# Attention of 24 score maps in one order of steps: scores a step earlier, one bias ahead of a division, even exponentials first

## Time and profile before

| | |
|---|---|
| runs of the kernel | 2519.49, 2513.41, 2519.65 us (median 2519.49) |
| profiled execution | 2518.29 us, its span 2516.5 us |
| granted clock of PE, mean | 0.999 |
| PE busy | 99% of the span |
| DVE, ACT, GpSimd busy | 61%, 54%, 10% |
| attention of layer 0 / layer 1 of block 2 | starts near 1562.7 / 2164.8 us of the span |

### The profile page before, as it was taken

How to read it: one execution, slowest core, us unless ns; L and a number is a source line. 1 busy time by engine, 2 the same in 40 slices (tenths; PEclk the granted TensorE clock), 3 DMA queues, 4 the chain that set the end, 5 groups by cost and what they waited for, 6 DMA issues and landing times.

```text
span 2516.5 us, 47973 instructions
## 1 busy us (share of the span) xinstructions
PE 2479.6 (99%) x19246; PEld 2312.7 (92%) x19246; DVE 1531.5 (61%) x2036; ACT 1346.9 (54%) x2077; POOL 255.5 (10%) x164
## 2 busy tenths in 40 slices
PE   9999999999999999999999999999999999999998
PEld 8989998999999999899989989799989988888997
DVE  5658756565565774656656556566555655567654
ACT  5447555544544664655555445665445445565543
POOL 0200220000000002100100001460000000354000
PEclk9999999999999999999999999999999999999999
DMA  6655414465655552348656555345555655434654
GB/s 235 207 186 172 136 67 160 143 197 195 198 198 193 168 166 70 126 142 228 205 178 202 194 177 161 110 145 187 188 189 186 195 193 168 135 111 167 201 188 139
DMA packets 118382, 428.10 MB, mean 170 GB/s; under 512 B 13164, under 2 KB 14956, under 8 KB 117804
## 3 DMA queue, kind: packets, MB, share of 16 engines
q1 hardware_dynamic: 117696, 424.82, 51.8%
q10 hardware_dynamic: 492, 0.46, 0.1%
HBM read 423.79 MB, written 1.44 MB: 169 GB/s over the span
## 4 chain that ended last, share of the span: by engine, by line
PE 92%; DVE 4%; ACT 2%; issue 1%; DMA 0%; ACTq 0%; SPq 0%; DVEq 0%; POOLq 0%
PE bank L483 41%; PE bank L694 39%; PE bank L503 2%; PE bank L1004 2%; PE bank L1708 1%; PE bank L1104 1%; DVE lo_slots L471 1%; PE bank L633 1%; PE bank L1725 1%; PE bank L1751 1%; PE bank L1895 1%; PE bank L1871 1%; DVE rope_mem L2108 1%; ACT hi_slots L457 0%; ACT probs L1790 0%
## 5 line engine op out<-in xcount | busy, mean ns | idle before, releaser
L471 DVE TENSOR_TENSOR lo_slots<-raw,hi_slots 128x1024 fp32r<-128x1024 f32 x732 | 901.1, 1237 | 696.3 <-ACT hi_slots L457 695.9
L457 ACT ACTIVATE hi_slots<-raw 128x1024 fp32r<-128x1024 f32 x788 | 830.7, 1058 | 737.2 <-PE bank L694 453.0
L694 PE MATMUL bank<-x_hi_room,hi_slots 128*128 128x256 f32 x2816 | 786.0, 279 | 1.7 <-DVE x_lo_room L663 1.2
L694 PE MATMUL bank<-x_lo_room,hi_slots 128*128 128x256 f32 x2816 | 784.1, 278 | 0.0
L694 PE MATMUL bank<-x_hi_room,lo_slots 128*128 128x256 f32 x2816 | 784.0, 278 | 0.0
L694 PEld LDWEIGHTS bank<-x_lo_room,hi_slots 128*128 128x128 f32 x2816 | 534.4, 190 | 0.1
L694 PEld LDWEIGHTS bank<-x_hi_room,hi_slots 128*128 128x128 f32 x2816 | 529.7, 188 | 3.9 <-issue 3.6
L694 PEld LDWEIGHTS bank<-x_hi_room,lo_slots 128*128 128x128 f32 x2816 | 530.0, 188 | 0.0
L483 PE MATMUL bank<-x_hi_room,hi_slots 128*128 128x256 f32 x1152 | 327.7, 285 | 1.9 <-DVE x_lo_room L663 1.4
L483 PE MATMUL bank<-x_lo_room,hi_slots 128*128 128x256 f32 x1152 | 319.7, 278 | 0.0
L483 PE MATMUL bank<-x_hi_room,lo_slots 128*128 128x256 f32 x1152 | 319.6, 277 | 0.0
(11 more groups left out here) (336 smaller groups left out, 3125.0 us busy)
## 6 DMA issues: line engine op xcount, KB each, us to landing
raw<-w_full SPq DMA_DIRECT2D x792, 512.0 KB, 4.1
bias_mem<-bias_rows SPq DMA_DIRECT2D x8, 288.0 KB, 6.4
mem<-mem_t SPq DMA_DIRECT2D x2, 1024.0 KB, 8.4
const<-consts SPq DMA_DIRECT2D x1, 1664.0 KB, 8.8
h<-x_t SPq DMA_DIRECT2D x2, 512.0 KB, 7.8
final<-finals SPq DMA_DIRECT2D x2, 512.0 KB, 6.4
out_t<-h SPq DMA_DIRECT2D x4, 256.0 KB, 2.7
bias_rows<-junk ACTq DMA_DIRECT2D x1, 384.0 KB
```

Of the source, the lines that this page charges most:

```text
L457: nc.scalar.activation(w_hi[s], raw[s][:, :], ACT.Copy).then_inc(hi_ready[s], 1)
L471: nc.vector.tensor_tensor(w_lo[s], raw[s][:, :], w_hi[s].bitcast(F32), ALU.subtract).then_inc(lo_ready[s], 1)
L694: mm = nc.tensor.matmul(out, lhsT=w[:, part], rhs=x[:, k, :], start=k == 0 and b % 2 == 0 and n == 0, stop=k == KT - 1 and b % 2 == 1 and ...
```

## The change

On PE the scores of a pair (i, i+1) with i of 2 or more are issued in step i-1, behind that step's transposes and values and ahead of its gate, not at the start of step i. On DVE the bias addition of an even map (kinds b and c) comes first in its step, ahead of the division of the map before. On ACT the exponentials of an even map come first in their step, ahead of the two copies; odd steps keep their order. The waits are the same ones, each at its instruction's new place.

```diff
+        def scores_early(maps, i):
+
+            return 2 <= i < len(maps) and i % 2 == 0
+
+        def pe_scores(E, maps, i):
+            two = maps[i:i + 2]
+            for n in range(i - 2 if i else 0, i):
+                if maps[n]["kind"] in "bc":
+                    pe.wait_ge(sems["s_bias"], E.after("s_bias", 2 * maps[n]["biased"] + 2))
+                else:
+                    pe.wait_ge(sems["s_exp"], E.after("s_exp", 2 * (n + 1)))
...
         def pe_attention(E, maps):
             probs, probs_t, _ = attention_tiles(E)
             for i in range(len(maps) + 2):
-                if i < len(maps) and i % 2 == 0:
-                    two = maps[i:i + 2]
...
+                if i < len(maps) and i % 2 == 0 and not scores_early(maps, i):
+                    pe_scores(E, maps, i)
...
+                if scores_early(maps, i + 1):
+                    pe_scores(E, maps, i + 1)
                 for g in gates_at(E, i):
                     pe_gate(E, g)
...
+            for i in range(len(maps) + 3):
+                first = i % 2 == 0
+                if first:
+                    exponential(i)
+                turned(i)
+                values(i)
+                if not first:
+                    exponential(i)
                 for g in gates_at(E, i - 1):
                     act_gate(E, g)
...
+            def add_bias(i):
+                m = maps[i]
+                dve.wait_ge(sems["s_ps"], E.after("s_ps", i + 1))
...
             for i in range(len(maps) + 4):
+                if scores_early(maps, i) and maps[i]["kind"] != "a":
+                    add_bias(i)
                 if 1 <= i <= len(maps):
                     m = maps[i - 1]
...
-                    dve.wait_ge(sems["s_ps"], E.after("s_ps", i + 1))
-                    if m["kind"] in "bc":
...
+                    if m["kind"] == "a":
+                        dve.wait_ge(sems["s_ps"], E.after("s_ps", i + 1))
+                    else:
+                        if not scores_early(maps, i):
+                            add_bias(i)
```

More of the change, by code:

```diff
@@ L1692, in act_gate @@
             split_hi(E, u)
+        def scores_early(maps, i):
[7 more added lines that the diff above has]
+                    pe.wait_ge(sems["s_exp"], E.after("s_exp", 2 * (n + 1)))
+            if i == 0:
+                pe.wait_ge(sems["pads"], E.after("pads", 1))
+            for t in range(TT):
+                for r, m in enumerate(two):
+                    mm = nc.tensor.matmul(bank[4 + r][:, tile_cut(t)], lhsT=m["q"][:, t * P:(t + 1) * P], rhs=m["k"],
+                                          start=True, stop=True)
+                    if t == TT - 1:
+                        mm.then_inc(sems["s_ps"], 1)
         def pe_attention(E, maps):
@@ L1762, in act_attention, with turned @@
             probs, probs_t, stat = attention_tiles(E)
-            for i in range(len(maps) + 3):
+            def turned(i):
                 if 1 <= i <= len(maps) and maps[i - 1]["use"] is not None:
@@ L1769, in act_attention, with values @@
                     nc.scalar.activation(probs_t[:, u % 2, :], bank[6 + u % 2][:, :], ACT.Copy).then_inc(sems["pt_sb"], 1)
+            def values(i):
                 if i >= 3 and maps[i - 3]["use"] is not None:
@@ L1780, in act_attention, with exponential @@
                                              ACT.Copy).then_inc(sems["y_hi"], 1)
+            def exponential(i):
                 if i < len(maps):
@@ L1805, in dve_attention @@
             probs, probs_t, stat = attention_tiles(E)
+            def add_bias(i):
+                m = maps[i]
+                dve.wait_ge(sems["s_ps"], E.after("s_ps", i + 1))
+                if i >= 3 and maps[i - 3]["use"] is not None:
+                    dve.wait_ge(sems["pt_ps"], E.after("pt_ps", maps[i - 3]["use"] + 1))
+                elif i >= 3:
+                    dve.wait_ge(sems["s_diff"], E.after("s_diff", maps[i - 3]["head"] - HEADS + 1))
+                for t in range(TT):
+                    at = (1 - t) * P
+                    nc.vector.tensor_tensor(probs[:, i % 3, tile_cut(t)], bias[:, m["head"], at:at + TOK],
+                                            bank[4 + i % 2][:, tile_cut(t)], ALU.add).then_inc(sems["s_bias"], 1)
             for i in range(len(maps) + 4):
+                if scores_early(maps, i) and maps[i]["kind"] != "a":
+                    add_bias(i)
                 if 1 <= i <= len(maps):
```

## The result

The changed kernel took 2549.78 us (median of 4 runs, 2548.03 to 2554.04), beside 2519.57 for the kernel before (4 runs, 2513.41 to 2520.39): 1.0137 times as long, with a 95% interval of 1.0117 to 1.0157. That is 34.5 us by the ratio (29.5 to 39.6), against the 27 forecast; the two medians lie 30.2 apart. The direction and the places were as forecast, but the loss is larger: 1.0137 times the time before is 2554, one microsecond above the range, though the median itself lies inside it.

A forecast was written before the change was run, and what follows sets the result against it. PE was taken to bound the kernel, so only its idle counts. Terms of 6.8 (no bias), 1.4 (bias and sink) and 5.3 (subtracted maps) make 13.5 us a layer, 27 over two layers: 2518.3 + 27 = 2545, range 2529 to 2553.

The forecast's parts named there:

- What bounds the kernel: Whole kernel: the matmul engine PE is busy 2479.6 of 2516.5 us, so reordering can win or lose nearly only its idle time.
- a sign of being wrong: Outside the two attention stages: a window changing by over a microsecond would count against the prediction.
- Kind a, +6.8 a layer: Attention maps without bias: early scores wait for the odd map's exponential, four PE idles of 1.7 us a layer.
- Kind b, +1.4 a layer: Maps with bias and sink: old idle goes, but GpSimd's split holds L1882; pairs take 10.77 us against 10.01.
- The bound of +2.5: Maps with bias and sink: upper limit of the loss in us a layer, another 0.3 for each pair.
- Kind c, +5.3 a layer: Maps with bias, two subtracted: GpSimd's split holds the subtraction; PE idles 1.5 for each of four pairs, less the old 0.7.
- That pushes L1825 to about 3.5 behind the start V: Two-map subtraction: the bias addition ahead of the division delays it to 3.5 us after the values start, split at V+3.15.
- ACT's order: Even exponentials ahead of ACT's copy delay copy and tanh by up to 1.2 us, at no cost to PE.
- without holds: Rival, 8%: GpSimd holds nothing in maps with bias, with or without subtraction; 2.0 us a layer, 2522.
- the faster one: Rival, 4%: in maps without bias the wait ahead of the odd gate costs nothing; -4.8 us a layer, 2509.
- the one with no hold in c: Rival, 20%: GpSimd's split doesn't hold the subtraction in two-map subtracted maps; 7.5 us a layer, 2533.
- Longer holds: Rival, 13%: division waits with the subtraction, 2.2 a pair; bias-and-sink pairs take 0.3 more; 17.2 us a layer, 2553.

## Where the prediction was right, and where it was wrong

*What bounds the kernel* held: the loss is PE's, in the two stages. Two things outside moved by over a microsecond all the same, which the prediction had named as a sign of being wrong. In the profiled executions the first scores came 3.7 us earlier after the change (1559.00 against 1562.67). That is the opening, where PE waits for its input; it varies between kernels that are alike up to there. And the stretch between the stages was 1.1 shorter, by the low clock shown above. The edit reaches neither.

*Kind a, +6.8 a layer:* shown. Eight idles, 13.8 us, each 1.69 or 1.74, on ACT's L1804.

*Kind b, +1.4 a layer:* the pairs took 10.77 to 10.80 us against 10.77 worked out, L1882 took 1.87 to 1.97 in 14 of 16 (the first of each layer, entered from kind a, 0.23), and the early order in kind b alone cost 1.6 and 1.7. The hold was taken off by itself, and a gain of 4 us a layer appeared. (The bound of +2.5 is a slip: 0.3 for each of three pairs makes 2.3, which the rival uses.) The idle ahead of the even transposes was 1.64, forecast 1.8.

*Kind c, +5.3 a layer:* the size was low and the cause was partly wrong. Idles of 1.41, 1.55, 1.55 and 2.01 stand in layer 0, 6.5 where 6.0 was forecast; L1863's mean is 1.7 and not over 2, since at half the places the division was held in its stead. By itself the kind cost 7.5 and 6.5, one low clock among them. "That pushes L1825 to about 3.5 behind the start V" gave the bias addition as the reason. With the bias put back the holds stayed, longer; with the copy put back they went. The step "*ACT's order* ... at nothing" was wrong therefore: it looked at who waits for the copy and the tanh, not at where the tanh lets the next split begin, which is what brings the two splits of a pair to 0.23 of each other.

*The step that failed* is the one that isn't in the sum: the clock was read at 1.00 before and left there, and "27" has no term for it. Four gates at the low level cost 6.2. The waits were sized well: 27.1 against 27, with kind a as forecast, kind b half a microsecond a layer lower and kind c as much higher. The forecast's idles of 1.5 to 1.7, sixteen in kinds a and c, should have raised the question of what PE's clock does behind them. The stage of the kernel before has no such idle, but the trace has two outside it, of 1.51 us, and behind one of them the clock is low for some 3.9 us. That gives both a price, up to 2 us, and a chance; for sixteen idles it would have been a term of several microseconds and a range that holds 2554.

*The rivals* without holds, the faster one and the one with no hold in c, fell by the timeline. "Longer holds" (2553) gave the time, for another reason: of its 3.7 a layer over the forecast 3.1 came as clock. That it came so near is luck.

## What to carry to other kernels

When a long instruction of one engine holds up another's, as GpSimd's splits do with DVE's here, an order is judged by where the long one starts: follow every reordered instruction to the one that releases it, and count the free time between two of them. An edit that gains nothing may be one half of a pair: here the early order and the narrow form of a two-element instruction, each within 0.1% of nothing, gained 0.4% together, and the same order cost in kinds a and c. And a sum that puts new idle on PE wants a term for its clock.

## What was not expected

- A TENSOR_SCALAR of 128x2 waits out the split (1.97 us); one of 128x1, started at the same place of a split, takes 0.21, and so do all sixteen of that kernel.
- The clock falls to the 1.2 GHz level behind some single idles of 1.5 to 2.8 us between busy stretches, and a gate then takes 4.3 instead of 2.8 us; with the waits filled by work nobody reads it stayed at 1.00.
- A held subtraction that starts 0.23 us behind the split takes 2.73 us: the whole of the split's rest and 0.5 more.
